# Attention in exact fp32 halves: stacked high/low operands, and a longer lag from scores to transposes

## The reference, cut to what matters

```
def chunk_attention(h, w_qkv, rel_bias, w_out):   # 16 heads of 64; chunks of 64 tokens
    q, k, v = split(h @ w_qkv)
    for each chunk c of queries: keys = its own chunk and the 8 before it
        s = q_c @ k_band.T * 64**-0.5 + bias(rel)
        p = softmax(s)            # over valid keys
        o_c = p @ v_band
    return o @ w_out
```

## Time and profile before

| | us |
|---|---|
| runs | 2795.66, 2800.63, 2800.87 |
| median | 2800.63 |
| profiled execution | 2796.26 |
| its span | 2794.2 |
| TensorE busy in the span | 2703.3 (97%) |
| VectorE busy | 1222.6 (44%) |
| ScalarE busy | 594.8 (21%) |
| GpSimd busy | 797.2 (29%) |

### The profile page before, as it was taken

How to read it: one execution, slowest core, us unless ns; L and a number is a source line. 1 busy time by engine, 2 the same in 40 slices (tenths; PEclk the granted TensorE clock), 3 DMA queues, 4 the chain that set the end, 5 groups by cost and what they waited for, 6 DMA issues and landing times.

```text
span 2794.2 us, 34049 instructions
## 1 busy us (share of the span) xinstructions
PE 2703.3 (97%) x12660; PEld 2222.7 (80%) x12660; DVE 1222.6 (44%) x1998; ACT 594.8 (21%) x1091; POOL 797.2 (29%) x450
## 2 busy tenths in 40 slices
PE   6999999989999999999899999999989999999997
PEld 5878888867888888888688888888768888888885
DVE  8225555575222223224745544445573333322225
ACT  3112112122000000001344443344530000000002
POOL 3223333243333333332201111111123333333335
PEclk9999999999999999999999999999999999999998
DMA  3223221111111111111100010011011111111101
GB/s 135 100 88 106 72 69 55 56 53 46 53 45 45 45 45 45 53 53 46 40 25 33 30 39 24 32 39 39 23 38 46 53 53 45 45 46 57 48 30 60
DMA packets 53220, 143.50 MB, mean 51 GB/s; under 512 B 5392, under 2 KB 15776, under 8 KB 53168
## 3 DMA queue, kind: packets, MB, share of 16 engines
q1 hardware_dynamic: 35632, 119.71, 12.4%
q10 hardware_dynamic: 17536, 23.07, 2.4%
HBM read 130.13 MB, written 12.63 MB: 51 GB/s over the span
## 4 chain that ended last, share of the span: by engine, by line
PE 46%; DVE 3%; issue 1%; ACT 1%; POOL 0%; DMA 0%; DVEq 0%; ACTq 0%; POOLq 0%; SPq 0%
PE bank L434 11%; PE bank L435 10%; PE bank L436 10%; PE scores L434 3%; PE scores L435 2%; PE scores L436 2%; PE probs_t L597 2%; PE probs_t L436 1%; PE probs_t L434 1%; PE probs_t L435 1%; DVE full L933 0%; DVE rstd L923 0%; PE bank L648 0%; DVE acc L915 0%; DVE prob L1157 0%
## 5 line engine op out<-in xcount | busy, mean ns | idle before, releaser
L434 PE MATMUL bank<-hn_hi,w_hi 128*128 128x512 f32 x2048 | 813.8, 397 | 23.6 <-DVE hn_lo L938 19.3
L436 PE MATMUL bank<-hn_hi,w_lo 128*128 128x512 f32 x2048 | 802.1, 392 | 0.0
L435 PE MATMUL bank<-hn_lo,w_hi 128*128 128x512 f32 x2048 | 801.1, 391 | 0.0
L352 POOL TENSOR_SCALAR w_hi<-raw 128x1024 fp32r<-128x1024 f32 x212 | 247.2, 1166 | 1933.1 <-PE bank L436 1359.0
L354 POOL TENSOR_TENSOR w_lo<-raw,w_hi 128x1024 fp32r<-128x1024 f32 x212 | 517.7, 2442 | 17.7
L434 PEld LDWEIGHTS bank<-hn_hi,w_hi 128*128 128x128 f32 x2048 | 386.6, 189 | 116.0 <-issue 15.4
L436 PEld LDWEIGHTS bank<-hn_hi,w_lo 128*128 128x128 f32 x2048 | 386.6, 189 | 82.3
L435 PEld LDWEIGHTS bank<-hn_lo,w_hi 128*128 128x128 f32 x2048 | 387.0, 189 | 78.0 <-issue 1.2
L1008 DVE TENSOR_TENSOR full<-bank,atmp 128x512 f32<-128x512 f32 x88 | 60.9, 691 | 715.7 <-ACT atmp L810 714.1
L810 ACT ACTIVATE atmp<-bank 128x512 f32<-128x512 f32 x88 | 52.6, 598 | 1152.5 <-PE bank L436 1152.5
L1017 DVE TENSOR_TENSOR x<-probs_t,x 128x512 f32<-128x512 f32 x240 | 162.7, 687 | 110.5 <-PE probs_t L436 110.3
(11 more groups left out here) (141 smaller groups left out, 3737.0 us busy)
## 6 DMA issues: line engine op xcount, KB each, us to landing
raw<-w_units_in SPq DMA_DIRECT2D x212, 512.0 KB, 3.2
v_raw<-v_scratch ACTq DMA_DIRECT2D x16, 512.0 KB, 4.1
bias<-rel_scratch ACTq DMA_DIRECT2D x8, 640.0 KB, 3.8
x<-x_t_in SPq DMA_DIRECT2D x16, 256.0 KB, 6.5
v_scratch<-atmp ACTq DMA_DIRECT2D x16, 256.0 KB, 2.5
v_scratch<-full ACTq DMA_DIRECT2D x16, 256.0 KB, 2.6
out_t<-x SPq DMA_DIRECT2D x16, 256.0 KB, 2.0
ws_raw<-w_s_t_in ACTq DMA_DIRECT2D x8, 64.0 KB, 1.8
```

The costliest lines, as they stand in the source:

```text
L352: pool.tensor_scalar(w_hi[slot][:, :], raw[r][:, :], 1.0, 1.0, ALU.mult, ALU.mult).then_inc(w_split, 1)
L434: pe.matmul(out, lh, rh, start=start, stop=False)
L435: pe.matmul(out, lh, rl, start=False, stop=False)
L436: last = pe.matmul(out, ll, rh, start=False, stop=stop)
```

## The change

Four things are done together.

1. Scores. `q2` holds, for each head, the high part on one half of the partitions and the low part on the other; `k2_hi` holds k's high part on both halves, `k2_lo` the low part on the head's half and zeros on the other. A piece is now two matmuls on 128 rows in place of three on 64. ACT writes two pieces of 64 partitions for a query half and four for a key half, where it wrote one; DVE writes two of each where it wrote one.
2. Values. `v2` holds the head's high part and low part side by side where `vz_hi` held the head and zeros. A key tile is two matmuls in place of three. `bank[3]` now holds two query tiles of both heads with high and low sums apart, so four times a pair ACT moves one half across partitions (`o_move`, into `o_side`) and DVE adds (`o_add`, into `o_full`), and `o_hi`, `o_lo` are made from `o_full` at steps 12 and 19 (before: 10 and 18).
3. Lags. Exponential one step behind the scores, reciprocal and scaling two, transposes and `pt_hi`/`pt_lo` three. 20 steps in place of 19, three `prob` buffers. TensorE does the scores of a step ahead of its transposes; `values` moves from even to odd steps; OUT0 starts at step 13.
4. The scratch that is set aside in SBUF for DMA descriptors is made 8192 bytes.

```diff
@@ tables @@
-        OUT0 = {11: (0,), 12: (1,), 13: (2,), 14: (3,), 15: (4,), 16: (5,), 17: (6,), 18: (7,)}
-        NEXT_Q = [{8: (0,), 9: (1, 2), 11: (3, 4), 13: (5, 6), 14: (7,)}, {16: (0,), 17: (1, 2, 3), 18: (4, 5)}]
+        OUT0 = {13: (0, 1), 14: (2,), 15: (3,), 16: (4,), 17: (5,), 18: (6,), 19: (7,)}
+        NEXT_Q = [{8: (0,), 9: (1, 2), 11: (3, 4), 13: (5, 6), 14: (7,)}, {16: (0,), 17: (1, 2), 18: (3, 4), 19: (5,)}]
+        LAG = 3
+        STEPS = 16 + LAG + 1
@@ TensorE @@
+                    pe.wait_ge(k2_zero, 2)
                 ge(pe, biased, it * 16 + s)
...
-                    product(scores[:, SHIFT + at:SHIFT + to], (q_hi[rows, tq], q_lo[rows, tq]), (k_hi[rows, tk], k_lo[rows, tk]),
-                            True, True, qk_done if to == WIN else None)
+                    pe.matmul(out, q2[:, head, tq], k2_hi[:, head, tk], start=True, stop=False)
+                    mm = pe.matmul(out, q2[:, head, tq], k2_lo[:, head, tk], start=False, stop=True)
...
-                if c % 4 == 0:
-                    ge(pe, o_lo_done, it * 2 + i // 4)
+                if c % 2 == 0:
+                    ge(pe, o_added, it * 8 + c)
...
-                    product(out, (vz_hi[:, key, head, :], vz_lo[:, key, head, :]), parts,
+                    pe.matmul(out, v2[:, key, head, :], parts[0], start=head == 0 and key == both[0][0] and n == 2, stop=False)
+                    mm = pe.matmul(out, v2[:, key, head, :], parts[1], start=False, stop=head == 1 and q == 1)
...
-                for m in range(19):
-                    if 0 <= m - 2 < 16:
-                        transpose_probs(it, m - 2)
+                for m in range(STEPS):
                     if m < 16:
                         scores_of(it, m)
+                    if 0 <= m - LAG < 16:
+                        transpose_probs(it, m - LAG)
...
-                    if m >= 4 and m % 2 == 0:
-                        values(it, m // 2 - 2)
+                    if m >= 5 and m % 2 == 1:
+                        values(it, (m - 5) // 2)
@@ ScalarE @@
+                def key_hi(h):
+                    act.wait_ge(p_done, p_number(it, "k", h) + 1)
+                    for to in range(2):
+                        for head in range(2):
+                            op = act.activation(k2_hi[rows_of(head if to == 0 else 1 - head), head, toks(h)],
+                                                p_bank(it, "k", h)[rows_of(head), :], ACT.Copy)
+                    op.then_inc(p_hi, 1)
+
+                def o_move(tiles):
+
+                    act.wait_ge(pv_done, it * 8 + (2 * tiles + 2))
+                    ge(act, o_added, it * 8 + 2 * tiles)
+                    for head in range(2):
+                        act.activation(o_side[rows_of(head), :], bank[3][rows_of(1 - head), head * 2 * P:(head + 1) * 2 * P],
+                                       ACT.Copy).then_inc(o_moved, 1)
...
+                    if m in (8, 12, 16, 19):
+                        o_move((m - 7) // 4)
@@ VectorE @@
             def query_lo(it, h, name="q", number=None):
...
+                for head in range(2):
+                    op = dve.scalar_tensor_tensor(flipped(q2[rows_of(1 - head), head, toks(h)]),
...
+                def o_add(tiles):
+                    ge(dve, o_hi_done, it * 2 + tiles // 2)
+                    dve.wait_ge(o_moved, it * 8 + (2 * tiles + 2))
+                    for head in range(2):
+                        rows = rows_of(head)
+                        dve.tensor_tensor(o_full[rows, tiles % 2 * 2 * P:(tiles % 2 + 1) * 2 * P],
+                                          bank[3][rows, head * 2 * P:(head + 1) * 2 * P], o_side[rows, :],
+                                          ALU.add).then_inc(o_added, 1)
...
-                        ge(dve, t_done, it * 16 + (m - 1))
+                        ge(dve, t_done, it * 16 + (m - 2))
```

More of the change, by code:

```diff
@@ L248, in trunk @@
             if pair < PAIRS - 1:
-                order[pair] += out_events("out0", 0, 3) + [(("q", 0), 2)] + out_events("out0", 3, KT) + [(("q", 1), 2)]
+                order[pair] += out_events("out0", 0, 2) + [(("q", 0), 2)] + out_events("out0", 2, KT) + [(("q", 1), 2)]
             else:
@@ L579, in scores_of @@
                 i, head = step(s)
-                rows = slice(head * HD, (head + 1) * HD)
                 if s == 0:
                     pe.wait_ge(p_read, p_number(it, "k", 1) + 1)
+                    pe.wait_ge(k2_zero, 2)
                 ge(pe, biased, it * 16 + s)
@@ L618, in values @@
                              for pt in (pt_hi, pt_lo)]
-                    product(out, (vz_hi[:, key, head, :], vz_lo[:, key, head, :]), parts,
-                            head == 0 and key == both[0][0] and n == 2, head == 1 and q == 1,
-                            pv_done if q == 1 else None)
+                    pe.matmul(out, v2[:, key, head, :], parts[0], start=head == 0 and key == both[0][0] and n == 2, stop=False)
+                    mm = pe.matmul(out, v2[:, key, head, :], parts[1], start=False, stop=head == 1 and q == 1)
+                    if q == 1:
+                        mm.then_inc(pv_done, 1)
             def attention(it, first, last):
@@ L838, in attention @@
                     query_hi(-1, 0)
-                    p_hi_part(it, "k", 0, k_hi[:, toks(0)])
+                    key_hi(0)
                     hi_tiles(2, 1)
@@ L863, in attention @@
                     if m in (1, 3):
-                        p_hi_part(it, "vt", m // 2, in_heads(vz_hi, m // 2), by_head(p_bank(it, "vt", m // 2)))
-                    if m == 15 and not last:
+                        p_hi_part(it, "vt", m // 2, v2_part(m // 2, False), by_head(p_bank(it, "vt", m // 2)))
+                    if m == 16 and not last:
                         load_bias(it + 1)
-                    if m in (10, 18):
-                        act.wait_ge(pv_done, it * 8 + (4 if m == 10 else 8))
-                        if m == 18 or not first:
-                            act.wait_ge(p_done, p_number(it, "out0" if m == 18 else "out1p", 7) + 1)
-                        act.activation(flipped(o_hi[:, :]), tiled(bank[3][:, :]), ACT.Copy).then_inc(o_hi_done, 1)
+                    if m in (8, 12, 16, 19):
+                        o_move((m - 7) // 4)
@@ L872, in attention @@
+                    if m in (12, 19):
+                        act.wait_ge(o_added, it * 8 + (4 if m == 12 else 8))
+                        if m == 19 or not first:
+                            act.wait_ge(p_done, p_number(it, "out0" if m == 19 else "out1p", 7) + 1)
+                        act.activation(flipped(o_hi[:, :]), tiled(o_full[:, :]), ACT.Copy).then_inc(o_hi_done, 1)
                     if m == 14 and not last:
                         query_hi(it, 0)
-                    if m >= 12 and last:
-                        square(3, 0, m - 12)
+                    if m >= 13 and last:
+                        square(3, 0, m - 13)
@@ L1129, in attention @@
                     keys_lo(1, 2)
-                    for part in (vz_hi, vz_lo):
-                        for head in range(2):
-                            dve.memset(r32(part[:, :, head, (1 - head) * HD:(2 - head) * HD]), 0.0).then_inc(vz_zero, 1)
+                    for head in range(2):
+                        dve.memset(r32(k2_lo[rows_of(1 - head), head, :]), 0.0).then_inc(k2_zero, 1)
                     mask_bias(0)
@@ L1173, in attention @@
                         out_add("out1p", 1, n)
-                    if m in (10, 18):
-                        dve.wait_ge(o_hi_done, it * 2 + (1 if m == 10 else 2))
-                        dve.tensor_tensor(flipped(o_lo[:, :]), tiled(bank[3][:, :]), flipped(r32(o_hi[:, :])),
+                    if m in (8, 12, 16, 19):
+                        o_add((m - 7) // 4)
+                    if m in (12, 19):
+                        dve.wait_ge(o_hi_done, it * 2 + (1 if m == 12 else 2))
+                        dve.tensor_tensor(flipped(o_lo[:, :]), tiled(o_full[:, :]), flipped(r32(o_hi[:, :])),
                                           ALU.subtract).then_inc(o_lo_done, 1)
```

118 lines of the change are left out of this document (68 added, 50 removed).

## The result

The changed kernel takes 2761.57 us (median of 4 runs, 2759.86 to 2763.3); the kernel before, on the same chip, 2798.42 (4 runs, 2795.66 to 2800.87). The ratio is 0.9869, with an interval of 0.9852 to 0.9886: faster by 1.3%. The forecast was 2755, its range 2725 to 2787. The profiled spans are 2794.2 and 2760.7 us, 33.5 less.

A forecast was written before the change was run, and what follows sets the result against it. TensorE's queue was taken to bound a body pair (busy 81.66 of 82.30 us). Gains 40 + 4 + 10 - 12 = 42 us from 2796.3 give 2754, plus 1 for a fast profiled execution: 2755, range 2725 to 2787.

The forecast's parts named there:

- Third matmuls: TensorE, each body pair: dropping the third matmul of each triple saves 3.7 us in scores and 4.2 in values.
- Change of rows: TensorE, body pair: ending switches between 64- and 128-row matmuls saves 0.37 us a step, 5.9 us for 16 steps.
- this term would be 0: Rival: the 64-row saving of 5.9 us a body pair does not come; 7 us gained, 2790; chance 0.04.
- Stalls: Body pair: TensorE waits where a step holds less work than the new chain's 2.5 to 2.7 us; 7.1 us lost.
- Net of a body pair: Each body pair: 13.8 us of removed TensorE time less 7.1 of waits, 6.7 gained; 40 us over six.
- Clock: Body pairs: TensorE's clock drops behind long waits, at 7 of 18 places, 1.7 us each; 12 us lost, bounds 0 and 31.
- The rival of a fall at every long stall: Rival, body pairs: the clock drops at each long wait, 31 us lost; 23 gained, 2774; chance 0.14.
- Its second price: Same rival if the clock stays low through steps 8 to 17: 5 us more a pair lost, gain near 0, 2790.
- First pair: First pair of heads: 4 us lost before its first scores, some 8 gained later; 4 gained (-3 to 10).
- Last pair: Last pair: step 9 transposes to second-half product fall from 32.8 to some 25 us, about 2 earlier; 10 gained (3 to 14).
- Moves across partitions: Rival: slow `o_move` and key moves hold up `values`; at 3 us a move, 2850; chance 0.06, shared with a longer chain.

The follow-up runs named there:

- the squares moved: Changed kernel, but in the last pair VectorE adds the squares ahead of `pt_lo`, not behind it: 2759.28 us, ratio 0.987 to the kernel before.
- the parts spread: Changed kernel, with parts of the next q moved from steps 9, 11 and 13 to steps 10 and 12: 2750.06 us, ratio 0.9833 to before.
- all four edits: Changed kernel: q parts mostly in steps 8, 10, 12; query parts at 15; step 16 output product first; `k2_lo` zeros early; squares before `pt_lo`: 2741.05 us.
- the zeros early: Changed kernel, with the memsets of `k2_lo`'s zero halves ahead of the first pair's second-half q parts: 2756.39 us, ratio 0.9857 to before.

## Why the prediction was right, and where not

- **Third matmuls, 7.9 us a body pair.** Right: 74.2 - 66.3 = 7.9.
- **Change of rows, 5.9.** Right in kind, too large: 5.0 where it was changed alone, 7.2 - 3.2 = 4.0 in the changed kernel. The 0.37 a step came from one step; another, on 128 rows, gave 1.70 - 1.43 = 0.27. One reading was wrong: I named 0.12 us for 256 columns as a distance on the full array, but those rows are on 64 rows, and the earlier trace rows has only 128 columns at 0.11. The timeline after bears the figure out, with 256-column scores on 128 rows at 1663.58, 1663.69 and 1663.82. The run with 128-row scores and the same columns was 0.5% faster, so 64-row scores are not the cheaper ones. By the rule of the Trainium skill (TensorE: Matmul & The Clock Gate, Packing small matmuls), weight loads overlap running matmuls only on other row groups; as I had applied it, this term would be 0, and these runs don't bear that out.
- **Stalls, 7.1.** By its parts: 8 to 9, 0.7 forecast and 0.7 found; 10 to 11, 1.4 and 1.4; 12 to 13, 1.5 and 1.6; 14 to 15, 0.15 and 0.26; 15 to 16, 2.0 and 1.8; 16 to 17, 0.5 and 0.5; steps 5 to 7, 0.65 and 0.6. The length of the chain was right; where it shows was not: I had the transposes of steps 11 and 13 wait for `pt_lo`, but it is the scores ahead of them that wait, for the bias. Moving the query's parts and the q parts removed the waits, which shows their causes.
- **Net of a body pair, 6.7.** 5.7 with the clock up. The rows' term was 1.9 too large, and 0.8 of that is made good by the waits that the kernel before already had.
- **Clock, 12 us lost.** The step that failed. Over the six body pairs it cost 1.1 us, in one of them. The same wait of 1.64 us stands in all of them, and only here do the transposes behind it take 1.14 us in place of 0.74:

```profile
1747.66 1.14 PE L607 MATMUL probs_t<-ident,prob 128*128 128x128 f32 x5 [1.64 <-DVE pt_lo L1211]
```

  I had priced it from one wait of the earlier trace rows, in the last pair, and taken 7 places of 18; why the clock falls behind one of these waits and not behind the others isn't shown. The rival of a fall at every long stall is out. Its second price was also added up wrongly: 23 gained less 5 for each of six pairs is 7 lost, 2804 and not 2790.
- **First pair, 4 gained.** It lost about 1: 5.7 up to the first scores (5.4 of them idle time, 6.80 for 1.41), where four key copies in a row (2.40) and the memsets (1.8, and 0.4 around them) cost more than my 4, and 4.7 gained behind, not 8. Its clock is 0.89 where it was 0.91.
- **Last pair, 10 gained.** The other step that failed: 1.9. From the transposes of s = 9 to the first `out1` product it takes 31.7 us, where it took 32.8 and I had some 25; the steps ahead of it gained 0.8, not 2. About half of the 6.7 us between 31.7 and 25 is the clock, which I had priced in the body pairs alone: with the clock at 1.00 and the squares moved, the same stretch takes 27.9. The other half is the chain, which is longer than I reckoned. ScalarE's squares stand ahead of the exponential and `pt_hi`, and wait for VectorE's sums:

```profile
1977.19 0.63 ACT L719 ACTIVATE atmp<-x 128x512 f32<-128x512 f32 x1 [1.12 <-DVE atmp L950]
...
1979.25 0.82 DVE L1211 TENSOR_TENSOR pt_lo<-probs_t,pt_hi 128x640 fp32r<-128x640 f32 x1 [1.49 <-ACT pt_hi L888]
...
1980.22 1.30 PE L607 MATMUL probs_t<-ident,prob 128*128 128x128 f32 x5 [2.15 <-DVE pt_lo L1211]
...
1993.59 0.80 PE L442 MATMUL bank<-o_hi,w_hi 128*128 128x512 f32 x1 [2.49 <-DVE o_lo L1229]
```

  Behind 2.15 us of idle time the transposes take 1.30: here the clock did fall. The squares' place is worth only 0.5 us, by the run that moved them. The last line shows another 1.0: the first `out1` product waits 2.49 us for `o_lo`, where it waited 1.47. No run takes the rest apart.
- **Moves across partitions.** Out: a move takes 0.38 us. In the changed kernel `values` wait for `o_full` nowhere in the first and the body pairs, and three times in the last (0.26, 0.58, 0.34). Once other waits are removed they do: once in a body pair with the parts spread (0.42), and with all four edits twice in each body pair (0.45 and 0.41) and in the first (0.54, 0.51).

So the total came as near as it did partly by luck, because errors cancel: the body pairs' clock was put 11 us too high, and the gains of the pairs were put too high as well, by 1.0 in each body pair, 5 in the first and 8 in the last. What the prediction did not see is that both halves of the change are needed: it priced the removed matmuls as a gain, the new order only by its stalls, and never asked what the old order's ring would have cost.

## What to carry to other kernels

When matmuls are taken from a software pipeline, look for the ring in the other engines' queues (here bias, exponential, high part, low part: 3.33 us) and compare it with what a step will hold afterwards; a deeper lag is worth nothing until then, and the shorter matmuls nothing without it. A new order needs its tables of filler work laid out anew: look for steps with nothing between the transposes and the next scores. Here the gains of moving work by a step or within one came out below what I expected (1.7 us a body pair of 3.1 for the parts, 1.0 of 1.4 for the query, 2.1 of at least 3.6 for all edits), because other waits took their place; so count what is next to wait before adding gains up.

## What the runs showed of the hardware

- Changing between 64- and 128-row matmuls costs 5.0 us in a body pair with 16 such blocks, some 0.3 us for each: here, scores on 128 rows with zeros in half of them were cheaper than on 64 rows.
- The same wait of 1.64 us was followed by a lower clock in one of six body pairs in both profiles of the changed kernel and in those with the squares moved and the parts spread, and in two of six with the zeros early. A fall lengthened the pair by 1.0 to 1.1 us. Why in that pair is open.
- Work on 64 partitions goes by its columns, and moving the result to the other 64 partitions costs nothing that shows. ScalarE takes 0.38 us for 256 columns (moved) and 0.59 for 512 (moved or not). VectorE takes 0.69 for 512 both for the query's low part, which is moved, and for the keys', which is not.
